# A two-part model on one core: the low halves of the hidden units move ahead of a tile's low half on VectorE, and products of zeros are put on TensorE ahead of eight kinds of stage

## The reference

```
def expert(acc, ew):
    wg, wu, wd, cw = ew
    hid = jax.nn.silu(t @ wg) * (t @ wu)
    return acc + (cw[:, None] * (hid @ wd)).astype(acc.dtype), None
```

## Time and profile before

| what | value |
|---|---|
| median of 3 runs | 2509.26 us (2508.42 to 2522.15) |
| profiled execution, its own time | 2514.59 us |
| its span, first to last instruction | 2512.9 us |
| TensorE busy, matmul / weight load | 2159.1 us (86%) / 1899.4 us (76%) |
| VectorE / ScalarE / GpSimd busy | 1591.7 us (63%) / 1115.9 us (44%) / 475.6 us (19%) |
| mean granted TensorE clock | 0.938 of full speed |

### The profile page before, as it was taken

The page is one execution under the profiler, slowest core; times in us unless marked ns, Lnnn a source line. Parts: engine busy times, 40 slices in busy tenths (PEclk is TensorE's granted clock), DMA queues, the critical chain, the costliest instruction groups (busy, mean ns, idle before and its releaser), DMA issues.

```text
span 2512.9 us, 40162 instructions
## 1 busy us (share of the span) xinstructions
PE 2159.1 (86%) x15258; PEld 1899.4 (76%) x15268; DVE 1591.7 (63%) x2540; ACT 1115.9 (44%) x1628; POOL 475.6 (19%) x328
## 2 busy tenths in 40 slices
PE   5999886788489776876899999889997999899997
PEld 2776465677377475765878999779996899888997
DVE  2878655577468555764566776666667666556665
ACT  3224533566333634674444455224332433455332
POOL 1000002688300016884042021100000000000000
PEclk7999898899789888998899999999998999999999
DMA  6457812799445136995325467455543445333452
GB/s 253 168 202 270 283 67 92 275 344 342 169 150 197 39 118 238 329 324 212 134 101 210 169 211 240 163 187 186 191 175 134 143 175 209 123 113 118 177 192 82
DMA packets 103173, 471.48 MB, mean 188 GB/s; under 512 B 11520, under 2 KB 30208, under 8 KB 66048
## 3 DMA queue, kind: packets, MB, share of 16 engines
q1 hardware_dynamic: 84480, 404.79, 45.4%
q0 software_dynamic: 13232, 44.84, 4.7%
q10 hardware_dynamic: 5328, 20.07, 2.0%
HBM read 412.76 MB, written 54.79 MB: 186 GB/s over the span
## 4 chain that ended last, share of the span: by engine, by line
PE 42%; DVE 6%; ACT 2%; issue 1%; DVEq 1%; SPq 1%; DMA 0%; POOL 0%; ACTq 0%; POOLq 0%
PE bank L754 12%; PE bank L756 12%; PE bank L755 12%; DVE ring_halves L424 2%; ACT high L1428 1%; PE bank L1149 1%; PE bank L1283 1%; PE bank L1335 1%; PE bank L805 1%; PE bank L1316 1%; PE bank L1273 1%; PE bank L1260 1%; DVE dring_halves L433 0%; PE bank L1265 0%; PE bank L1264 0%
## 5 line engine op out<-in xcount | busy, mean ns | idle before, releaser
L754 PE MATMUL bank<-ssdb_halves,high 128*128 128x256 f32 (+1 forms) x2080 | 619.5, 298 | 51.1 <-DVE HT_halves L1967 18.6
L755 PE MATMUL bank<-HT_halves,high 128*128 128x256 f32 (+1 forms) x2096 | 619.6, 296 | 0.0
L756 PE MATMUL bank<-ssdb_halves,ring_halves 128*128 128x256 f32 (+1 forms) x2080 | 616.6, 296 | 0.0
L424 DVE TENSOR_TENSOR ring_halves<-ring,high 128x2048 fp32r<-128x2048 f32 (+1 forms) x230 | 482.3, 2098 | 195.6 <-ACT high L1428 194.4
L1428 ACT CAST high<-ring 128x2048 fp32r<-128x2048 f32 x230 | 437.5, 1903 | 217.6 <-PE bank L756 121.2
L754 PEld LDWEIGHTS bank<-ssdb_halves,high 128*128 128x128 f32 x2080 | 396.2, 190 | 70.7 <-issue 37.1
L755 PEld LDWEIGHTS bank<-HT_halves,high 128*128 128x128 f32 x2096 | 402.1, 192 | 8.9
L756 PEld LDWEIGHTS bank<-ssdb_halves,ring_halves 128*128 128x128 f32 x2080 | 396.5, 191 | 10.3
L424 POOL TENSOR_TENSOR ring_halves<-ring,high 128x1024 fp32r<-128x1024 f32 x66 | 224.7, 3404 | 651.7 <-ACT high L1428 651.7
L433 DVE TENSOR_TENSOR dring_halves<-dring,dhigh 128x1024 fp32r<-128x1024 f32 (+1 forms) x152 | 226.3, 1489 | 159.6 <-ACT dhigh L1434 159.1
L1434 ACT CAST dhigh<-dring 128x1024 fp32r<-128x1024 f32 x152 | 160.6, 1057 | 243.9 <-PE bank L756 243.9
(11 more groups left out here) (453 smaller groups left out, 3888.1 us busy)
## 6 DMA issues: line engine op xcount, KB each, us to landing
ring<-in_ffn SPq DMA_DIRECT2D x88, 1024.0 KB, 5.6
ring<-in_moe SPq DMA_DIRECT2D x64, 1024.0 KB, 7.4
ring<-in_ada SPq DMA_DIRECT2D x48, 1024.0 KB, 6.1
dring<-in_ffn_down SPq DMA_DIRECT2D x88, 512.0 KB, 3.7
dring<-in_moe_down SPq DMA_DIRECT2D x64, 512.0 KB, 4.7
ring<-in_foxin SPq DMA_DIRECT2D x24, 1024.0 KB, 4.9
ring<-in_win SPq DMA_DIRECT2D x22, 1024.0 KB, 7.7
zs_b<-x_slots POOLq DMA_DIRECT2D x32, 512.0 KB, 8.9
```

What stands on the lines that cost most here:

```text
L424: eng.tensor_tensor(low, w, h, ALU.subtract).then_inc(sem(f"low_{engine}"), 1)
L754: mm(o, a[0], b[0], start=first, stop=last and bool(kw), **kw)
L755: mm(o, a[0], b[1], start=False, stop=last and bool(kw), **kw)
L756: return mm(o, a[1], b[0], start=False, stop=last, **kw)
```

## The change

Two parts.

1. In `experts.one` of VectorE, `make_low` for tile `j + 2` moves from its place behind L2395 to the place behind L2399. So it now stands ahead of `split_rows` and `make_down_low`, and it is the low part of the hidden units that goes first.
2. `filler` becomes `idle_products(n, bank)`, callable from everywhere in TensorE's program. The calls inside `s5()` keep their numbers (8 and 6, bank 6). New calls stand ahead of eight kinds of stage, with the numbers in `IDLE`: 24 ahead of `win` in layer 0 (0 in layer 1), 10 ahead of each `wout`, 8 ahead of each router, 40 and 54 between `tokens` and the experts, 46 ahead of each wait for `y_sum`, 24 ahead of the first `fox`, 22 ahead of `glu`, 28 ahead of `pooling`. In all there are 320 new products of 128 x 128 zeros by 128 x 512 zeros. They wait for nothing themselves.

```
+IDLE = {"win": (24, 0), "wout": 10, "rt": 8, "moe": (40, 54), "sum": 46, "fox": 24, "glu": 22, "pool": 28}
...
+            def idle_products(n, bank):
+
+                for _ in range(n):
+                    mm(ps[bank][:], zeros[:, 0:P], zeros, start=True, stop=True)
...
                 ada(l + 1, ADA_PARTS[l + 1][0], ADA_AHEAD[l])
+                idle_products(IDLE["win"][l], 5)
...
             def moe(l, blocks):
                 tokens(l, blocks)
+                idle_products(IDLE["moe"][l], 5)
                 experts(("moe", l), EXPERTS)
...
                 pe.wait_ge(sem("out_taken"), base("out_taken", ("over", l)) + OVER)
+                idle_products(IDLE["sum"], 5)
                 for b in range(blocks):
...
-                def filler(n):
-
-                    for _ in range(n):
-                        mm(ps[6][:], zeros[:, 0:P], zeros, start=True, stop=True)
-
                 inputs(0)
-                filler(8)
+                idle_products(8, 6)
                 for c in range(KC):
                     if c + 1 < KC:
                         inputs(c + 1)
-                    filler(6)
+                    idle_products(6, 6)
                     outputs(c)
+                idle_products(IDLE["glu"], 6)
...
+                idle_products(IDLE["wout"], 5)
                 wout(l, tok)
                 mean_square(("ffn", l), tok)
+                idle_products(IDLE["rt"], 6)
                 router(l, 2 if last else 4)
                 moe(l, TB if last else 2 * TB)
             mean_square(("final1",), slice(0, T))
+            idle_products(IDLE["fox"], 6)
...
                     mean_square(("pool",), slice(0, T))
+                    idle_products(IDLE["pool"], 6)
                     pooling()
...
                     dve.wait_ge(sem("gate_act"), act0 + j + 1 + RING * g)
                     tt(hrows[:, j % 2, :], gact[:, j % 2, 0:P], ps[4 + j % 2][:, P:TCOLS], ALU.mult).then_inc(sem("hid_raw"), 1)
-                    if j + 2 < slices:
-                        make_low(dve, "dve", c0 + j + 2, g)
                     dve.wait_ge(sem("hid_high"), hid_high0 + j + 1 + RING * g)
                     tt(r(hid[:, j % 2, 1, 0:P]), ps[4 + j % 2][:, TCOLS:TCOLS + P], hid[:, j % 2, 0, 0:P], ALU.subtract)\
                         .then_inc(sem("hidden"), 1)
+                    if j + 2 < slices:
+                        make_low(dve, "dve", c0 + j + 2, g)
                     if j % 2 == 0 and j // 2 + 1 < blocks:
                         split_rows(j // 2 + 1, g)
```

## The result

The changed kernel takes 2630.76 us (median of 4, 2629.74 to 2636.77), against 2509.43 us for the kernel before beside it. The ratio is 1.0476 [1.0439, 1.0513]: slower by 120 us. The forecast was 2581 us, so the sign was right and the size 50 us short. The time lies 36 us above the end of the range. The changed file is 9 lines longer: L2399, L2390, L2395, L424, L433, L1079 and L1062 of before are now L2406, L2399, L2404, L425, L434, L1086 and L1069, and ScalarE's copies of the block's result, L1646 before, are L1655. (L1646 of the changed file is L1637 of before, the high copy of the rows.)

The account below looks back on a forecast made before the run. The loop was taken as bound by copies, gate activation, high copy, the low tile's second half, gate_up and the odd down. 2514.6 + 77 - 5 = 2586.6 us profiled, 2581 us for the median; range 2500 to 2595.

Parts of the forecast that it names:

- Part 1, even slice: Expert loop: VectorE's low half waits for GpSimd's, split_rows queues behind it, next gate_up starts at 8.68, 1.25 us later.
- GpSimd's duration of 2.4 us: Sign in the even slices: GpSimd's low half lasts 2.4 us; staying at 3.4 us would make the forecast wrong.
- Part 1, odd slice: Expert loop: GpSimd's next low half gets the shared port ahead of VectorE's down half; turn_hidden at 11.54, another 1.33 us lost.
- The first rival: Odd slice: VectorE gets the port, so only 1.25 us a block are lost, 2541 us; chance 0.33.
- The second and third rivals: Even slice, VectorE's low half not held: GpSimd stretched instead, 2504 us, chance 0.15; or neither held, 2486 us, chance 0.07.
- from there to `down` it is 1.53 us as before: Odd slice: the stretch from turn_hidden to down keeps its earlier length of 1.53 us.
- The block price: Expert loop: a block takes 14.67 us instead of 12.09; 30 x 2.58 = +77 us.
- Part 2: Products ahead of stages: they fit in idle time and raise the clock, -5 us, between 0 and -23, +7 by overrun.
- its whole bound of 2.9 us: Sixteen matmuls behind layer 1's sum: a higher clock gains at most 2.9 us; less than half was counted.
- The two places ahead of the experts: Products between tokens and the experts, one place per layer: a gain of 1.9 us each by the clock.
- a clock of 1.00 at the starts of the experts: Sign for the products: TensorE runs at full clock when each layer's experts start.
- I take no overrun: All new products end within their idle times; ahead of y_sum, 46 take 9.9 us of 15.1 us.

Follow-up runs that it names:

- e8_no_pool: Changed kernel without the new products, and VectorE makes every low part by itself, none on GpSimd: 2523.86 us, ratio 1.0028 to the kernel before.
- e4_move_warm2: Changed kernel without products ahead of stages, but with 40 products of 128 columns in each odd slice's TensorE wait: 2598.93 us, ratio 1.0333 to the kernel before.
- e2_products_only: Changed kernel with VectorE's order put back as before, all 320 products kept: 2505.52 us, ratio 0.9965 to the kernel before.
- e1_move_only: Changed kernel with the move of the low half alone, no new products: 2637.26 us, ratio 1.0488 to the kernel before.
- e6_odd_only: Kernel before with the new order in the odd slices alone, no products: 2516.22 us, ratio 0.9993 to the kernel before.
- e7_best2: Changed kernel without products, split_rows ahead of the low half, VectorE taking 1408 of 2048 columns and all of the down tile's: 2551.91 us, ratio 1.0146.
- e9_no_pool_old: Kernel before, its order kept, with VectorE making every low part by itself, none on GpSimd: 2550.4 us, ratio 1.0133 to the kernel before.
- e3_split_first: Changed kernel without products, with split_rows ahead of the tile's low half on VectorE: 2529.31 us, ratio 1.0056 to the kernel before.

## Why the prediction was right or wrong

*Part 1, even slice: right.* The steps, counted from the start of ScalarE's copies (574.40), forecast and measured: the hidden units' low half done 4.27 and 4.26; GpSimd's low half done 6.25 and 6.25; VectorE's 7.34 and 7.33; `split_rows` 8.54 and 8.52; `gate_up` 8.68 and 8.58. GpSimd's duration of 2.4 us was the sign I had named for right. By the row, VectorE's 3.15 us is a wait for GpSimd's end (580.65) and then 1.08 us of its own work. It is so in the whole loop: but for the first block of each layer, each of VectorE's even passes takes 3.14 to 3.16 us. The Trainium skill, SBUF — State Buffer, section "SBUF: two separate sides", says that of the two the one that comes second is blocked until the first has ended. The trace agrees: the end worked out that way was 7.34, and it came at 7.33.

*Part 1, odd slice: right.* GpSimd got the port for its next half, by 0.02 us. Its half is done at 10.80 (forecast 10.74), VectorE's down half at 11.34 (11.29), and `turn_hidden` starts at 11.60 (11.54). The first rival (VectorE gets it) occurred in no block: in all 30 GpSimd's instruction starts 0.02 to 0.04 us ahead, and VectorE's takes 2.88 to 2.90 us. But the forecast had put a chance of 0.33 on that rival and called the race one of 0.1 us, so the outcome was a guess that came true, not a step that was worked out. The second and third rivals (VectorE is not held up; where the prediction speaks of the third and fourth, it means these) are out by the same rows and by e8_no_pool.

*The step that failed: "from there to `down` it is 1.53 us as before".* It was 2.83 us (586.00 to 588.83), and from `down` to the next copies 2.54 us instead of 1.60. That is the 2.3 us between 14.67 and 16.97, and it is the clock: in e4_move_warm2, where it stayed at 1.00, both take 1.60 us (547.94 to 549.54 and on to 551.14). I took the block's TensorE time at the 1.00 of the earlier trace rows, though I had myself put waits of 1.2 and 1.3 us more into each block. No term and no rival asked what the clock does when the loop's waits grow; I asked it only for part 2. e4_move_warm2 sizes the term: ratio 1.0488 without products in the wait, 1.0333 with them, 39 us. In the changed kernel it is 2.15 us for a block in layer 0. In layer 1 it is less: its blocks take 14.9, 16.4 and 17.2 us there. In e4_move_warm2, at the full clock, they take 14.9 and 16.4 us in turn (12.2 and 13.7 us in the kernel before), so only the three of 17.2 us lost clearly.

*The block price: right, a little small.* 30 x 2.58 = 77 us was forecast; at a held clock it is 2.7 us a block in both layers (from `turn_rows` to `turn_rows`: 14.9 less 12.2 in layer 0, 15.6 less 12.9 in layer 1), 81 us.

*Part 2: right in sign, the size within its bounds, but two of its terms are wrong.* -5 us was forecast, -9 us measured by itself. L811 behind layer 1's sum gave back its whole bound of 2.9 us, where I had counted less than half. The two places ahead of the experts, counted at 1.9 us each, gave nothing that can be seen. The products held the clock at 1.00 while they ran, but it fell again behind them, before `gate_up` had begun, and the first `gate_up` of both loops still runs at 0.50 in the changed kernel. So the sign "a clock of 1.00 at the starts of the experts" did not come:

```profile
457.00:461.00 4.00, 4.00 (x20) 4.00 (x20) 0.00 (x0) 0.00 (x0) 0.00 (x0) 0.50 0.16 65
1033.00:1037.00 4.00, 4.00 (x20) 4.00 (x20) 0.00 (x0) 0.00 (x0) 0.00 (x0) 0.50 0.20 75
```

"I take no overrun" was wrong for layer 1's `y_sum`, by 2.8 us in e2_products_only. Where the rest of the 9 us comes from was not taken apart. Within the changed kernel the products can hardly be seen (1.0476 with them, 1.0488 without, intervals that overlap), so there the -5 us of the sum has no run behind it. TensorE's wait ahead of `y_sum` is down from 31.3 to 1.1 us and that for the first row load from 29.2 to 6.0 us, since the products stand there now.

*The sum.* 2509 + 81 (VectorE's lateness at a held clock) + 39 (clock) is 2629 us for the move alone, where e1_move_only's ratio gives 2632. In part this is a circle, for the 39 us are the difference of two ratios, and only the 81 us are counted by themselves. The profiled executions give both without it: from the first to the last `turn_rows`, both loops together take 365 us before, 440 us in e4_move_warm2 and 474 us in e1_move_only. That is 75 us for the lateness, in 28 of the 30 blocks, and 34 us for the clock, 26 of them in layer 0. The range's upper end allowed 0.3 us more for each block; the clock took seven times that in layer 0.

*Open.* In the profiled execution of the changed kernel the first loop starts 3.5 us later than before (its first `turn_rows` is at 452.07 against 448.61 us). In e1_move_only, e4_move_warm2 and e6_odd_only it is 6 us later, though nothing of the move lies ahead of it, and in e7_best2, e8_no_pool and e9_no_pool_old it is not later at all. e6_odd_only is no slower for it. No run took this apart. It is open, too, why the same waits bring the clock down in one block and not in another. With waits of 1.27 and 0.40 us in a block of 12.1 us it stayed at 1.00; with 1.55 us in 12.5 us (e3_split_first) and 1.66 us in 12.4 us (e8_no_pool) it did so in all blocks but one, the first of each loop apart; with 1.95 us (e7_best2) it fell in some blocks. With 2.55 us and 0.7 to 1.0 us (1.3 us where the clock is held) it fell in each block of layer 0 from the fourth on, but in less than half of layer 1's, where waits of 1.71, 2.55 and 1.32 us stand in the row 1130.90 to 1147.30 at 1.00. e4_move_warm2 shows that the second wait alone does not do it; no run has the first wait without the second.

## What to carry to other kernels

When a change lets TensorE wait longer inside a loop that ran at the full clock, price the loop twice: at that clock, and with the matmuls behind the wait at the lower one. Here the forecast was right to 0.1 us up to the second wait, and still 50 us short of a loss of 121 us, 34 to 39 of them by the clock.

Before moving an instruction of VectorE behind another, look at what GpSimd runs at that moment. A subtraction of two SBUF operands that starts 0.3 us behind GpSimd's pays for all of GpSimd's, and so does everything queued behind it. Put operations that read PSUM into GpSimd's time, and the SBUF ones at its end: that swap was worth 4.3% here (e3_split_first). Where both engines share a job only to halve it, try it with VectorE alone, and try it in both orders: here it cost 0.3% in the new order, where the shared version cost 4.9%, but 1.3% in the old order, where the shared version is the kernel before.

## What the runs showed that was not expected

- VectorE alone is quicker with the whole than beside GpSimd with half: 2.28 us for 2048 columns against 3.15 us for 1024, 1.21 us for 1024 against 2.89 us for 512.
- The clock fell and came back within a block, over and over: 6.8 us at 0.50 in a block of 16.97 us, in the loop of layer 0. In layer 1 the same waits left more than half of the blocks at 1.00. Forty products of 128 columns (2.41 us) in a wait of 2.6 us kept it at 1.00 in all but the first block of each loop.
- Products ahead of a stage do not help its start when they end too early: with 4.1 and 1.9 us between the last product and the first `turn_rows`, and another 2.6 us behind it, the first `gate_up` of both loops ran at 0.50 as before.
- Two subtractions issued 0.02 us apart differ by who waits: GpSimd's took 2.37 us, as it does alone, and VectorE's 2.89 us for 512 columns, of which some 0.5 us are its own.
- A change in the even slices alone reproduces the whole loss (1.0481 against 1.0488), and one in the odd slices alone none of it (0.9993), although over a quarter of the new waiting is in the odd ones.
